# Splitting 512-column products into two of 256 columns, in passes of six

## What is computed

```python
h = h + fox_mixer(rms_norm(h, mix_norm), fox_w_in, ...)        # out: mix @ w_out
h = h + conv_ffn(rms_norm(h, ffn_norm), w_up, ..., w_down)     # 2048 -> 2 x 5632 -> 2048
x = x + mix @ w_out            # mix = gla_mixer(...) beside dilated_mixer(...)
x = x + (silu(h2 @ w_gate) * (h2 @ w_up)) @ w_down             # 2048 -> 2 x 5632 -> 2048
```

## Time and profile before

| | |
|---|---|
| median of 3 runs | 2248.68 us (2247.97 to 2249.47) |
| span of the profiled execution | 2248.4 us |
| TensorE busy | 2236.0 us, 99% |
| weight loads busy | 1962.7 us, 87% |
| VectorE busy | 1614.3 us, 72% |
| ScalarE busy | 1215.8 us, 54% |
| products, and as many weight loads | 13,082 |
| moved from HBM | 419.0 MB, 188 GB/s |

### The profile page before, as it was taken

How to read it: one execution, slowest core, us unless ns; L and a number is a source line. 1 busy time by engine, 2 the same in 40 slices (tenths; PEclk the granted TensorE clock), 3 DMA queues, 4 the chain that set the end, 5 groups by cost and what they waited for, 6 DMA issues and landing times.

```text
span 2248.4 us, 38811 instructions
## 1 busy us (share of the span) xinstructions
PE 2236.0 (99%) x13082; PEld 1962.7 (87%) x13082; DVE 1614.3 (72%) x2397; ACT 1215.8 (54%) x1585; POOL 53.5 (2%) x78
## 2 busy tenths in 40 slices
PE   8999999999999999999999999999999999999999
PEld 6888888888888888888888888888888888888888
DVE  8787777888888888555567677777676666665554
ACT  7777765655555555444465577655444444443333
POOL 1111100000000000000000000000000000000000
PEclk9999999999999999999999999999999999999999
DMA  6555555555555555555545555555555555556664
GB/s 225 188 178 185 186 175 190 190 195 194 187 187 195 192 191 193 194 193 192 191 156 190 164 178 168 170 196 194 188 192 189 191 191 196 191 192 199 204 198 138
DMA packets 118602, 421.99 MB, mean 188 GB/s; under 512 B 13773, under 2 KB 15973, under 8 KB 118544
## 3 DMA queue, kind: packets, MB, share of 16 engines
q1 hardware_dynamic: 114048, 413.66, 55.7%
q0 software_dynamic: 2048, 5.42, 1.0%
q10 hardware_dynamic: 2448, 2.11, 0.3%
HBM read 419.01 MB, written 3.70 MB: 188 GB/s over the span
## 4 chain that ended last, share of the span: by engine, by line
PE 99%; DMA 1%; DVE 0%; SPq 0%; ACT 0%; issue 0%
PE acc L415 59%; PE acc L424 29%; PE acc L412 3%; PE b_val L412 2%; PE acc L421 2%; PE b_val L421 1%; PE b_score L478 0%; PE b_turn L483 0%; DMA xres<-xt 0%; DMA raw<-wstream 0%; PE b_mean L491 0%; PE b_score L477 0%; PE b_mean L471 0%; PE b_mean L472 0%; PE b_mean L492 0%; PE b_mean L493 0%
## 5 line engine op out<-in xcount | busy, mean ns | idle before, releaser
L753 ACT ACTIVATE w<-raw 128x1024 fp32r<-128x1024 f32 x783 | 824.8, 1058 | 807.7 <-PE acc L424 769.9
L1064 DVE TENSOR_TENSOR w<-raw,w 128x1024 fp32r<-128x1024 f32 x783 | 959.2, 1228 | 382.4 <-ACT w L753 379.6
L415 PE MATMUL acc<-xs,w 128*128 128x512 f32 x3832 | 992.5, 394 | 0.6 <-DVE xs L1087 0.4
L415 PEld LDWEIGHTS acc<-xs,w 128*128 128x128 f32 x3832 | 676.6, 188 | 108.5 <-issue 1.2
L424 PEld LDWEIGHTS acc<-xs,w 128*128 128x128 f32 x3832 | 532.4, 188 | 55.7
L424 PE MATMUL acc<-xs,w 128*128 128x256 f32 x3832 | 542.3, 277 | 0.0
L415 PE MATMUL acc<-hid,w 128*128 128x512 f32 x1408 | 360.1, 392 | 0.0
L1070 DVE TENSOR_REDUCE folded_t<-acc 128x256 f32<-128x512 f32 x324 | 223.0, 688 | 116.7 <-PE acc L424 94.6
L415 PEld LDWEIGHTS acc<-hid,w 128*128 128x128 f32 x1408 | 247.4, 188 | 37.8
L424 PEld LDWEIGHTS acc<-hid,w 128*128 128x128 f32 x1408 | 194.2, 188 | 19.8
L424 PE MATMUL acc<-hid,w 128*128 128x256 f32 x1408 | 197.6, 277 | 0.0
(11 more groups left out here) (205 smaller groups left out, 1234.0 us busy)
## 6 DMA issues: line engine op xcount, KB each, us to landing
raw<-wstream SPq DMA_DIRECT2D x783, 512.0 KB, 3.3
decay_row<-decay_scratch POOLq DMA_DIRECT2D x16, 128.0 KB, 3.5
out<-xres ACTq DMA_DIRECT2D x16, 128.0 KB, 2.9
xres<-xt SPq DMA_DIRECT2D x3, 512.0 KB, 7.6
dist_scratch<-bias_scratch POOLq DMA_DIRECT2D x8, 192.0 KB, 4.7
toeplitz<-dist_scratch POOLq DMA_DIRECT2D x8, 128.0 KB, 3.8
xres<-xt SPq DMA_DIRECT2D x2, 256.0 KB, 3.6
raw<-wstream SPq DMA_DIRECT2D x2, 256.0 KB, 4.4
```

The source lines that it names most:

```text
L415: pe.matmul(acc[bank_no][:, :], w_hi, x[:, kc, :, :].rearrange("p a s -> p (a s)"), start=opens, stop=False)
L753: act.activation(whi[slot][:, :], raw[slot][:, :], ACT.Copy).then_inc(hi_ready, 1)
L1064: dve.tensor_tensor(wlo[slot][:, :], raw[slot][:, :], whi[slot][:, :], ALU.subtract).then_inc(lo_ready, 1)
```

## The change

A new kind of size, `Thirds(n)`, handles n blocks in three passes of n short products each: `w_hi` with x high into the left half of the bank, `w_hi` with x low into the right half, `w_lo` with x high into the right half. It is used behind the three opening groups in the last stretch of `project`, in the loop of `up` and in that of `down`. The openings stay as they are, and so does everything else in the kernel.

```diff
+class Thirds:
+    def __init__(self, n):
+        self.n = n
...
             def stretch(pos, blocks, x, *sizes):
...
-                for longs, shorts in sizes:
+                for size in sizes:
+                    if isinstance(size, Thirds):
+                        assert behind == at
+                        thirds(pos, blocks[at:at + size.n], x)
+                        at = behind = at + size.n
+                        continue
+                    longs, shorts = size
...
+            def thirds(pos, blocks, x):
+                for k, j, bank_no, kc, opens, closes, free, late in blocks:
+                    if j == 0:
+                        pe.wait_ge(lo_ready, pos.unit(k) + 1)
+                    if free is not None:
+                        pe.wait_ge(chunk_out, free)
+                    if late:
+                        pe.wait_ge(*late)
+                    w_hi = whi[pos.slot(k)][:, j * P:(j + 1) * P]
+                    pe.matmul(acc[bank_no][:, 0:S], w_hi, x[:, kc, 0, :], start=opens, stop=False)
+                for k, j, bank_no, kc, opens, closes, free, late in blocks:
+                    w_hi = whi[pos.slot(k)][:, j * P:(j + 1) * P]
+                    pe.matmul(acc[bank_no][:, S:2 * S], w_hi, x[:, kc, 1, :], start=False, stop=False)
+                for k, j, bank_no, kc, opens, closes, free, late in blocks:
+                    w_lo = wlo[pos.slot(k)][:, j * P:(j + 1) * P]
+                    mm = pe.matmul(acc[bank_no][:, S:2 * S], w_lo, x[:, kc, 0, :], start=False, stop=closes)
+                    if j == BLOCKS - 1:
+                        mm.then_inc(unit_used, 1)
...
-                stretch(pos, units(1, 0, 8) + units(2, 0, 8) + units(3, 0, 8), mix, *SETTLE, *[6] * 29)
+                stretch(pos, units(1, 0, 8) + units(2, 0, 8) + units(3, 0, 8), mix, *SETTLE, *[Thirds(6)] * 29)
...
-                    stretch(Pos(layer.unit_up + 8, 24, i), units(3 * i + 1, 0, 24), xs, *SETTLE, *[6] * 29)
+                    stretch(Pos(layer.unit_up + 8, 24, i), units(3 * i + 1, 0, 24), xs, *SETTLE, *[Thirds(6)] * 29)
...
-                    stretch(pos, blocks, hid2, *SETTLE, *[6] * 53, 8, 8)
+                    stretch(pos, blocks, hid2, *SETTLE, *[Thirds(6)] * 55, Thirds(4))
```

More of the change, by code:

```diff
@@ L397, in stretch @@
             def stretch(pos, blocks, x, *sizes):
-                sizes = [size if isinstance(size, tuple) else (size, size) for size in sizes]
-                assert all(sum(part) == len(blocks) for part in zip(*sizes))
+                sizes = [size if isinstance(size, (tuple, Thirds)) else (size, size) for size in sizes]
                 at = behind = 0
-                for longs, shorts in sizes:
+                for size in sizes:
[5 more added lines that the diff above has]
+                    longs, shorts = size
                     for k, j, bank_no, kc, opens, closes, free, late in blocks[at:at + longs]:
@@ L427, in stretch @@
                     behind += shorts
+                assert at == behind == len(blocks)
+            def thirds(pos, blocks, x):
[16 more added lines that the diff above has]
+                        mm.then_inc(unit_used, 1)
             def half(pos, k, bank_no, part, x, late=None):
```

## The result

The changed kernel takes 2255.49 us (median of 9) against 2248.85, a ratio of 1.0029 with a 95% interval of 1.0020 to 1.0038: slower, and 13 us over the forecast. One of the nine runs took 12,743 us in a slow state, for a reason that no trace shows, and the ratio leaves it out. On another occasion the median was 2254.67, ratio 1.0028 (1.0015 to 1.0041). Its profiled execution has a span of 2251.5 us, 3.1 more than that of before. In the new kernel's rows, line 427 is a long product, line 436 a short one of the old kind, and lines 452, 455 and 458 are the three passes; queue q8 brings instruction packets.

A forecast was written before the change was run, and what follows sets the result against it. The prediction took TensorE, busy 99% of the span, to bound the kernel. From 2248.7 us it took off 9.4 for the passes and added 3.2 for down's two loop edges: 2242.5 us, range 2238.5 to 2248.

The forecast's parts named there:

- The bound and the passes: TensorE sets the time; in project, up and down, 18 shorts take 2.040 us a group against 2.0534, without new waits.
- The term of 9.4 us: Gain from the passes: 9.1 us over 676 groups in project, up and down, plus 0.3 us at down's ends.
- The loop edge of down: Down's longer loop body may not be kept, so each branch back waits for code: 1.6 us each, two 3.2.
- Its own sign of being wrong: At down's two loop edges: the prediction called itself wrong if they took over 4 us each.
- The cover of 1.93 us: At down's branch back, seventeen short products already ahead of the branch cover 1.93 us, less than the 2.86 of before.
- 0.5 + 3.0: At down's branch: 0.5 us for a kept branch holding the sequencer, plus 3.0 us for fetching an instruction packet.
- A dearer edge: Rival, chance 0.12: down's edges cost 5 to 11 us through a 5.4 us fetch, second wait or low clock; 2244 to 2250.
- the slow pace: Rival, chance 0.10 in a good part: changed stretches run shorts at 117.5 ns; in all groups 41.6 us more, with edges 2293.
- The body that is kept: Rival, chance 0.22: down's longer loop body is kept after all, no wait at the edge, 2239.3 us.
- fixed cost for each product: Rival, chance 0.05 together with slow issue: six more products a group at 6.6 ns each take 27 us, 2276.
- the case without any gain: Rival, chance 0.05: the long product's 2.3 ns come back between the passes; 2248.7 us, with the edges 2252.
- The base: Start of the sum for the whole kernel: 2248.7 us, the median of the runs; profiled span 2248.4, 0.3 us around it.

The follow-up runs named there:

- the straight version: The changed kernel with down's two passes written out one behind the other, so no branch back: 2238.82 us, ratio 0.9959 against the kernel before.
- the hint: The changed kernel, loop kept, with the sequencer told at the head of each pass of down where the branch will go: 2240.39 us, ratio 0.9964.
- the run with 1788 products and loads: The changed kernel with 24 groups of down's loop left as six longs and shorts, then 31 of three passes: 2251.17 us in one execution.
- the pair with four and three: Changed kernel, down written out, plus one group of four longs and shorts, or three and three, before each down stretch's passes: 2258.30 and 2238.67 us.
- the first two experiments: Changed kernel with down left as before: 2242.74 us, ratio 0.9972; changed kernel with down's two passes written out: 2238.82 us, ratio 0.9959.

## Why the prediction was wrong

*The bound and the passes* were right. TensorE set the time, 18 shorts take 2.040 us in place of 2.0534, the new halves cost what the old ones did, issue kept up inside the passes, and no wait for another engine came. The term of 9.4 us is 9.3 by the start stamps (6.2 and four times 0.78); the medians of before and the straight version differ by 9.9 (2248.73 less 2238.82).

*The loop edge of down* was the right mechanism, and its price is the term that the sum had wrong: 3.2 us for the two edges, where the stamps show 3.1 for layer 0 and 12.4 for layer 1. Its own sign of being wrong, edges of over 4 us, came in layer 1 alone. Part of the miss is the stop itself. The cover of 1.93 us was met: in layer 0 the branch began at 1000.65 by its stamp and the products ran out at 1002.57. From the branch to the first product behind it the hold was 4.8 and 5.2 us where 0.5 + 3.0 was taken. The fetch was priced by the landing of a small DMA; the packet itself started only 2.2 us into the branch (2.5 in layer 1), took 0.9 us, and 1.4 us more passed until the branch was done. So 2.9 and 3.2 us of standing instead of 1.6 each: 3.0 us of the miss.

*The rivals were taken as alternatives, and that is the step that failed:* it kept the edge's price to the stop alone. A dearer edge (0.12) and the slow pace (0.10) were given chances of their own, as if one or the other came. The prediction names the branch as one place where the pace can be lost, and adds the plain edges to that rival, but it puts the second wait, the low clock and the pace into no common sum. They came together: behind the stop of layer 1 a second stop, a low clock and an opening that ends slow all stood, in both traces of the changed kernel, 9 us on top of the first stop, and without the stop (straight, or with the hint) none of them did in down. The range ended at 2248, at most of the dear edge alone; with two slow second passes of 55 groups at 75 ns added to that rival's 2250, it would have reached 2258.

*On the slow pace* the price was nearly right: 13.4 + 61.6 = 75 ns a group against the fast pace, 4.1 us in a pass of 55, where 990 shorts at 117.8 instead of 113.3 ns cost 4.4. It took no more than one pass of down in four. Three things in its reasoning were wrong. The slow pace doesn't only follow a stop or products of another kind: the slow eight at 1004.46 in the earlier trace rows stand behind eight longs and nothing else. Long products don't end the slow pace by themselves: in the run with 1788 products and loads, layer 1's second pass had 24 groups of six longs and six shorts behind a slow opening, and all of them stayed slow (the chain):

```profile
2128.87 1.37 PE acc L427 x6
2130.24 0.71 PE acc L436 x6
2130.95 1.37 PE acc L427 x6
2132.32 0.71 PE acc L436 x6
```

It is the count of longs that leads out of the fast pace, as the pair with four and three shows, and the counts of longs and shorts that lead back. So a slow pass isn't special to passes of shorts; by these 24 groups the old form would have kept it too, though no run has a whole pass of it. And "every opening ends fast" held for the entries of before; an entry behind a stop of 3 us at a low clock is one that it doesn't always repair. Why it does in one case and not in another is open.

*No fixed cost for each product* showed, and the case without any gain is refuted by the first two experiments. The body that is kept, the rival at 2239.3, was wrong of this kernel (nine packets or more come in each second pass); the straight version has the time that it would have had, 2238.8.

*The base* held: the runs of before were 2248.1 to 2248.9 in the median throughout. That 0.3 us lie around the span was wrong: where time and span of one execution are both known it is 1.8 us (2238.36 and 2236.5 in the straight version), so by that before's profiled execution was 1.5 us slower than its median, with its low clock at 1145. The sum started from the median and isn't touched by it.

## What to carry to other kernels

Count the instructions of a loop's body on the engine that sets the time before an edit that multiplies them: here a body that was held branched back in 0.2 us, one that wasn't waited 3.6 to 4.8 us for code, and what covers that is only the work already queued. Write such a loop out, or give the branch a hint, and the edit's own gain comes through. And where one stop can set off several prices (another fetch, a lower clock, a worse pace), add them in one case instead of giving each a chance of its own.

## What the hardware showed

- TensorE's instruction packets: loop bodies of 1408 products and loads were held, 1668 once and once not, 1788 to 2076 never; without the hint a branch was quick behind a pass with five or six instruction packets and slow behind one with seven to nine.
- A branch to code that isn't held keeps the sequencer 3.6 to 4.8 us, against 0.21 where it is held and 0.35 to 0.40 with a hint. With 17 products ahead of the branch, all of them shorts, TensorE stands 2.1 to 3.2 us.
- The granted clock fell behind 7 of the 11 such stops in the traces, for 3.4 us, or 6.8 where a second stop followed.
- 256-column fp32r products with a weight load each run at 113.3 or at 117.7 ns. Shorts keep their pace for as long as they run (990 in a row here), three or six 512-column products keep the fast pace and four or eight end it; behind six shorts at the slow pace, six keep it slow.
